# Two-block transformer step, first expert layer: results of 14 of its 16 experts placed by accumulating indirect DMA instead of by matrix products

## The chip, the cores and the metric

The kernel runs on one core of a Trainium2 chip; the other cores are idle. The metric is the device time of one execution in microseconds (us). Three executions of the kernel before took 3236.24, 3239.30 and 3238.56 us, median 3238.56. One more execution was profiled.

The core's engines work side by side: PE (matrix products, with its weight loads PEld), DVE (vector), ACT (scalar), POOL (GpSimd) and SP, which here only issues weight loads. Semaphores tie them together. All DMA queues of the core share 16 DMA engines.

## What is computed

The reference runs two layers of a hybrid attention block, then two layers of a second block. The change is in the expert stage of the second block's first layer (layer 0), where both the 512 latent tokens and the 256 context tokens go through 16 experts:

```python
def expert_choice_ffn(h, router_w, w_gate, w_up, w_down):
    B, n, D = h.shape                        # n = 512 (latent) or 256 (context), D = 1024
    cap = EC_CAPACITY * n // N_EXPERTS       # 64 or 32 tokens for each of 16 experts
    aff = jax.nn.softmax((h @ router_w).astype(F32), axis=-1)
    gate, idx = lax.top_k(jnp.swapaxes(aff, 1, 2), cap)
    xe = jax.vmap(lambda hb, ib: hb[ib])(h, idx)
    a = jnp.einsum('becd,edf->becf', xe, w_gate)
    u = jnp.einsum('becd,edf->becf', xe, w_up)
    ye = jnp.einsum('becf,efd->becd', jax.nn.silu(a) * u, w_down) * gate[..., None].astype(h.dtype)
    return jax.vmap(lambda ib, yb: jnp.zeros((n, D), h.dtype).at[ib.reshape(-1)].add(yb.reshape(-1, D)))(idx, ye)

lat = lat + mod_l[5] * expert_choice_ffn(h_l, ...)      # and the same for the context
```

Each expert picks its 64 best latent tokens; its 64 result rows are scaled by their gates and added into the rows of those tokens. A token can be picked by several experts, but only once by each. Everything is float32. The weights of one expert are three 1024 x 1024 matrices, 12 MB in all.

## The kernel before

The program is a row of phases. In each, every engine runs its own function, and semaphores (`S[...]`, `wait_ge`) order them; no scheduler moves anything. The residual stream lies turned in the memory of the core: `XT` holds it as 8 blocks of 128 channels by 512 tokens, `CT` the same for the context.

**Weights.** `Stream.load` (L275) on SP loads the weights in pieces of 1 MB, in the order in which PE uses them. In this layer a ring of 13 pieces is used, somewhat more than the 12 of one expert. A load waits until the piece that lay in its place is used (`w_used`). The ring's last two places hold the token rows before, so their first loads also wait until these are stored: `if OPENED[self.n] == FIRST_OPEN + 1: self.e.wait_ge(S["rows_kept"], 16 * 6)`.

**The gate phase.** `pool_first_gate` (L2467) stores the 768 token rows into the DRAM array `KEPT` (named token_rows in the trace), in six DMAs (L2477). `dve_top` and `dve_select` make selection matrices for four experts at a time.

**The expert loop on PE** (`pe_moe_both`, L2718). For an expert e: half of the context products (L2740), the latent products with gate and up weights (L2727), the other half of the context products; then `pe_turn` turns the hidden values (L2804), `pe_turn_ctx` the context's (L2797); then the down products, latent (L2770) and context (L2779). Between these stand small jobs, planned in `Moe.plan` (L1959) and issued by `pe_aux` (L2562) at two spots: (e, 0) lies between `pe_turn` and `pe_turn_ctx`, (e, 1) right before the down products. "first" and "last" lie before and behind the loop. The kinds of jobs:
- x, xc: the inputs of the next four experts, turned from rows that POOL gathered from `KEPT` (L2580); emptied by ACT.
- i: token numbers and gates of four experts as columns in PSUM (L2571, L2574); emptied by DVE (L2655 to L2662) into `SHARE` (gates), `PLACE` and `ROWS` (token numbers).
- y: the results of a pair of experts into all tokens, one job for each of the 8 blocks of channels. It is a product of the 128 result rows `YE` with a 128 x 512 matrix `G` that holds the gate where row and token belong together (L2601). DVE multiplies it by the modulation and adds it to `XT` (L2648).
- yc: the same for the context, four experts at a time (L2606, L2666).

The y jobs of a pair run during the two experts that come next, four in each, in experts 2 to 15; the eight of the last pair run in "last". The jobs at the inner spots take turns on three PSUM banks: `inner = (2, 3, 6) if s.ctx`. `pe_aux` waits until the job that last used the bank has been emptied.

**DVE** (`dve_moe_d`): `product` (L2868) multiplies the two halves of the hidden values, `copy` (L2863) and `product_ctx` (L2873) serve the context, `dve_aux` empties its jobs, `pair_map` (L2896) makes `G`. **ACT** (`act_moe_d`): the silu, the copy of the turned hidden values (L2829), and the copies of an expert's 64 result rows into `YE` (L2852), which end with `e_ready`. **POOL** (`pool_experts`): nine indirect gathers of 128 rows each (L2489), three for each of the groups 1 to 3 of four experts.

The second layer has a loop of its own, `pe_moe_d`, which keeps its y jobs.

## Time and profile before

| | |
|---|---|
| three executions, us | 3236.24, 3239.30, 3238.56 |
| the profiled execution, us | 3236.32 |
| its span from first to last instruction, us | 3234.5 |
| PE busy in the span | 3049.3 us, 94% |
| DVE, ACT, POOL busy | 47%, 22%, 10% |
| granted TensorE clock, mean | 0.981 of full speed |
| layer 0's expert loop, start of expert 0 to end of "last" | about 1801.8 to 2408.6 us |

The profile comes from one execution. Its span plus what lies around it is that execution's time, 3236.32 us, which is 2.24 us under the median of the three. Times in the rows are counted from the start of the span. A float32 product stands in the trace as two MATMUL instructions (a transposition as one), so the 128 y products of both layers are 256 instructions. An instruction's duration includes the time in which it overlaps its neighbours; the distance from start to start tells what it really costs.

### The profile page before, as it was taken

To read this page: it belongs to the slowest core of one execution; us is meant where nothing else is said; L and a number is where in the kernel's file an instruction comes from. 1 tells how busy PE (TensorE), PEld (TensorE's weight loads), DVE (VectorE), ACT (ScalarE), POOL (GpSimd) and SP (SyncE) were. 2 spreads that over 40 slices of the span, in tenths; PEclk is the share of its full clock that TensorE was granted. 3 is DMA by queue.
4 is the path that set the end of the run, shared out by engine and by line. 5 is a ranking of instruction groups with operands and counts; after the bars stand their busy time and mean duration, and the time that the engine had idled before them with its cause. 6 is when DMAs were issued, how large, how long until landed. Compare 5 with 4: busy or idle time off the path is not lost.

```text
span 3234.5 us, 36328 instructions
## 1 busy us (share of the span) xinstructions
PE 3049.3 (94%) x14559; PEld 1675.0 (52%) x14559; DVE 1526.7 (47%) x2852; ACT 726.6 (22%) x1521; POOL 330.1 (10%) x195
## 2 busy tenths in 40 slices
PE   8999899998989899999998999999999888899998
PEld 5888443787744344456755533333335544444443
DVE  5993942998482434765565222222243762111112
ACT  1211532121262211121124100000014652111111
POOL 4553000655200000000001000000000000000000
PEclk9999999999999899999999999999999999999999
DMA  5442003455201222010412798888841003999997
GB/s 221 169 183 96 10 1 125 158 192 225 79 1 39 106 81 107 33 52 30 161 65 93 331 376 338 351 343 331 348 176 52 27 3 138 379 421 421 421 421 294
DMA packets 87625, 598.23 MB, mean 185 GB/s; under 512 B 10456, under 2 KB 11259, under 8 KB 16932
## 3 DMA queue, kind: packets, MB, share of 16 engines
q1 hardware_dynamic: 79776, 575.70, 44.5%
q10 hardware_dynamic: 5524, 12.35, 1.1%
q0 software_dynamic: 2160, 7.87, 0.6%
q8 instruction: 117, 1.92, 0.2%
q14 instruction: 48, 0.39, 0.0%
HBM read 590.64 MB, written 5.24 MB: 184 GB/s over the span
## 4 chain that ended last, share of the span: by engine, by line
PE 63%; DVE 7%; ACT 2%; issue 1%; another core or an unknown queue 0%; DVEq 0%; ACTq 0%; PEldq 0%
PE ps L1358 8%; PE ps L2727 7%; PE ps L2689 7%; PE ps L2706 3%; PE ps L2770 3%; PE ps L2740 3%; PE ps L2601 3%; PE ps L1091 3%; PE ps L3013 2%; PE ps L2584 2%; PE ps L2779 2%; PE ps L2500 2%; PE ps L1456 2%; PE ps L1696 2%; PE ps L3174 1%; PE ps L1508 1%
## 5 line engine op out<-in xcount | busy, mean ns | idle before, releaser
L610 PE MATMUL ps<-mem 128*128 128x256 f32 x1792 | 393.3, 381 | 12.7 <-DVE mem L640 10.8
L610 PEld LDWEIGHTS ps<-mem 128*128 128x128 f32 x1792 | 340.2, 191 | 65.2 <-DVE mem L640 14.7
L555 POOL TENSOR_TENSOR mem<-mem 128x512 f32<-128x512 f32 (+1 forms) x160 | 302.0, 1887 | 544.4 <-DVE mem L851 284.8
L2868 DVE TENSOR_TENSOR mem<-ps,mem 128x512 f32<-128x512 f32 x32 | 22.1, 692 | 547.0 <-PE ps L2689 313.4
L753 DVE SCALAR_TENSOR_TENSOR mem<-mem 128x1024 f32<-128x1024 f32 x160 | 255.3, 1635 | 13.4 <-DMA mem<-in_ada_w 13.4
L1358 PE MATMUL ps<-mem 128*128 128x512 f32 (+1 forms) x768 | 253.5, 492 | 2.9 <-ACT mem L1199 2.9
L2727 PE MATMUL ps<-mem 128*64 128x512 f32 x1024 | 223.3, 594 | 0.0
L2689 PE MATMUL ps<-mem 128*64 128x512 f32 x1024 | 222.5, 592 | 0.7 <-ACT mem L2626 0.7
L1358 PEld LDWEIGHTS ps<-mem 128*128 128x128 f32 x768 | 147.1, 193 | 108.6 <-issue 97.2
L640 DVE TENSOR_TENSOR mem<-ps,mem 128x256 f32<-128x256 f32 x308 | 121.2, 418 | 111.8 <-PE ps L610 68.3
L1091 PE MATMUL ps<-mem 128*128 128x512 f32 x384 | 169.6, 597 | 1.8 <-DVEq L156 1.8
L2727 PEld LDWEIGHTS ps<-mem 128*64 128x64 f32 x1024 | 72.1, 137 | 150.5 <-issue 150.5
L2689 PEld LDWEIGHTS ps<-mem 128*64 128x64 f32 x1024 | 74.4, 137 | 145.6 <-issue 144.6
L608 PE MATMUL ps<-mem 128*128 128x256 f32 x672 | 146.3, 379 | 1.5 <-POOL mem L555 1.5
L608 PEld LDWEIGHTS ps<-mem 128*128 128x128 f32 x672 | 127.6, 190 | 19.2 <-issue 1.9
L2601 PE MATMUL ps<-mem 128*128 128x512 f32 x256 | 117.3, 596 | 1.7 <-ACT mem L2852 1.3
L1091 PEld LDWEIGHTS ps<-mem 128*128 128x128 f32 x384 | 71.5, 190 | 88.3 <-issue 85.6
L2740 PE MATMUL ps<-mem 128*32 128x512 f32 x1024 | 116.1, 594 | 0.0
L2706 PE MATMUL ps<-mem 128*64 128x512 f32 x512 | 113.4, 595 | 1.1 <-ACT mem L2829 1.1
L2770 PE MATMUL ps<-mem 128*64 128x512 f32 x512 | 113.4, 595 | 0.0
L2648 DVE SCALAR_TENSOR_TENSOR mem<-ps,mem 128x512 f32<-128x512 f32 x128 | 96.0, 750 | 33.2 <-PE ps L2601 22.2
L2852 ACT ACTIVATE mem<-ps 64x512 f32<-64x512 f32 x64 | 37.9, 592 | 294.2 <-PE ps L2770 153.9
(412 smaller groups left out, 4071.5 us busy)
## 6 DMA issues: line engine op xcount, KB each, us to landing
mem<-in_moe_w SPq DMA_DIRECT2D x384, 1024.0 KB, 14.0
mem<-in_w_in SPq DMA_DIRECT2D x48, 1024.0 KB, 8.3
mem<-in_ada_w SPq DMA_DIRECT2D x48, 1024.0 KB, 4.9
mem<-in_hy_w_in SPq DMA_DIRECT2D x24, 1024.0 KB, 7.0
mem<-in_w_out SPq DMA_DIRECT2D x12, 1024.0 KB, 6.9
mem<-in_k_win_l SPq DMA_DIRECT2D x8, 1024.0 KB, 6.9
mem<-in_hy_w_out SPq DMA_DIRECT2D x8, 1024.0 KB, 4.9
mem<-in_sw_w_in SPq DMA_DIRECT2D x6, 1024.0 KB, 7.2
```

Source lines behind the costliest of these rows:

```text
L555: gp(out, x, y, op).then_inc(A.mark(sem), 1)
L608: m = mm(seven(l, unit), y[:, k, u * P:(u + 1) * P], x[:, k, :], start=(k == 0), stop=(k == 3))
L610: m = mm(seven(l, unit), x[:, k, :], y[:, k, :], start=(k == 0), stop=(k == 3))
L753: stt(PRODUCT if again else w, w, 1.0, C_ROWS[:, z, :], ALU.mult, ALU.mult, accum_out=mod(layer, b // KD, b % KD, z))\
L1091: m = mm(ps[:, b, :], Wr[slot[n]][:, k, b * P:(b + 1) * P], GT[:, 4 * c + k, :], start=(n == 0 and k == 0), stop=(n == 2 and k == 3))
L1358: m = mm(ps[:, j % 4, 0:L], Wc[s][:, k, (j % 4) * P:(j % 4 + 1) * P], H[:, k, :], start=(k == 0), stop=(k == KD - 1))
L2601: m = mm(ps[:, bank, :], m_.YE[i % len(m_.YE)][:, j * P:(j + 1) * P], m_.G, start=True, stop=True)
L2689: m = mm(ps[64 * x:64 * x + 64, part, :], lat(k), w[x][:, k % 4, :], start=(k == 0), stop=(k == KD - 1))
L2706: m = mm(ps[64 * x:64 * x + 64, 7, :], m_.AT[:, k, :], w[x][:, k % 4, :], start=(k == 0), stop=(k == KD - 1))
L2727: m = mm(ps[64 * x:64 * x + 64, part, :], m_.XS[e // GROUP % 2][:, k, e % GROUP, 0:CAP_L], w[x][:, k % 4, :], start=(k == 0), stop=(k == K ...
L2740: m = mm(ps[32 * i:32 * i + CAP_C, 4, :], m_.XS[e // GROUP % 2][:, k, e % GROUP, CAP_L:], w[i][:, k % 4, :], start=(k == 0), stop=(k == KD ...
L2770: m = mm(ps[64 * x:64 * x + 64, 7, :], m_.AT[:, k, :], w[k // 4 * 2 + x][:, k % 4, :], start=(k == 0), stop=(k == KD - 1))
```

## The change

1. In layer 0 the y jobs of pairs 0 to 6 (experts 0 to 13) are gone: 56 jobs. The eight of pair 7 stay in "last".
2. POOL, after the six stores of token rows, sets a tile to zero and stores it four times into a new DRAM array `ADDED` (512 x 1024). SP's wait on `rows_kept` and POOL's now include these four stores.
3. For each of experts 0 to 13, `add_rows` issues one indirect DMA on POOL: the 64 rows of `YE` are added to 64 rows of `ADDED`, whose numbers stand in the new `TARGET`. It waits for the expert's `e_ready` and for the add before it. The gathers of groups 2 and 3 stand in POOL's order before the adds of experts 3 and 7.
4. After the last add POOL loads `ADDED` into four tiles `BACK`. Eight new "back" jobs in expert 15 (two at (15, 0), six at (15, 1)) turn them, four transpositions each, and DVE adds each to `XT` by the instruction that empties a y job.
5. In layer 0 `product` multiplies by the gate, which now has a row for each slot in the new `GATE`; it was `tensor_tensor` and is `scalar_tensor_tensor`, with a wait on DVE's own last instruction. `G` holds ones in place of gates. Emptying an i job takes 19 tiny instructions in place of 11, and the i job of experts 0 to 3 moves from (0, 1) to "first".
6. ACT writes experts 0 to 13 alternately into two `YE` tiles, always in partitions 0 to 63, and waits from expert 2 to 14 for the add of the expert two before.

PE, one expert of the layer's loop in the middle (expert 4). Before:

```order
L2740 MATMUL ps<-mem 32x512 x16
L2804 MATMUL ps<-mem 128x128 x4
L2580 MATMUL ps<-mem 128x128 x4
L2797 MATMUL ps<-mem 128x128 x4
L2601 MATMUL ps<-mem 128x512 x4
L2606 MATMUL ps<-mem 128x256 x2
L2770 MATMUL ps<-mem 64x512 x16
```

The same place in the changed kernel, whose lines are numbered anew (L2840 is `pe_turn`, L2609 the x job, L2833 `pe_turn_ctx`, L2639 yc, L2806 the down products):

```order
L2776 MATMUL ps<-mem 32x512 x16
L2840 MATMUL ps<-mem 128x128 x4
L2609 MATMUL ps<-mem 128x128 x4
L2833 MATMUL ps<-mem 128x128 x4
L2639 MATMUL ps<-mem 128x256 x2
L2806 MATMUL ps<-mem 64x512 x16
```

The four y products have gone and nothing has taken their place.

PE at the end of the layer, from the last hidden products of expert 15. Before:

```order
L2740 MATMUL ps<-mem 32x512 x16
L2804 MATMUL ps<-mem 128x128 x4
L2601 MATMUL ps<-mem 128x512 x2
L2797 MATMUL ps<-mem 128x128 x4
L2601 MATMUL ps<-mem 128x512 x2
L2606 MATMUL ps<-mem 128x256 x2
L2770 MATMUL ps<-mem 64x512 x16
L2779 MATMUL ps<-mem 32x512 x16
L2601 MATMUL ps<-mem 128x512 x8
L2606 MATMUL ps<-mem 128x256 x8
```

The same place in the changed kernel (L2634 are the "back" transpositions, L2630 the y products that stay):

```order
L2776 MATMUL ps<-mem 32x512 x16
L2840 MATMUL ps<-mem 128x128 x4
L2634 MATMUL ps<-mem 128x128 x8
L2833 MATMUL ps<-mem 128x128 x4
L2634 MATMUL ps<-mem 128x128 x24
L2639 MATMUL ps<-mem 128x256 x2
L2806 MATMUL ps<-mem 64x512 x16
L2815 MATMUL ps<-mem 32x512 x16
L2630 MATMUL ps<-mem 128x512 x8
L2639 MATMUL ps<-mem 128x256 x8
```

Four products make way for 32 transpositions; "last" is as it was.

POOL, from the stores of token rows to the end of the layer in the changed kernel (before, only the rows of token_rows stood here, the nine gathers one behind another):

```order
L2483 DMA token_rows<-mem 128x1024 x6
L2485 MEMSET mem 128x1024
L2488 DMA added_rows<-mem 128x1024 x4
L2518 DMA mem<-token_rows,mem 128x1024 x3
L2496 DMA added_rows<-mem 512x1024 x3
L2518 DMA mem<-token_rows,mem 128x1024 x3
L2496 DMA added_rows<-mem 512x1024 x4
L2518 DMA mem<-token_rows,mem 128x1024 x3
L2496 DMA added_rows<-mem 512x1024 x7
L2508 DMA mem<-added_rows 128x1024 x4
```

The gathers (L2518) of groups 2 and 3 now stand behind three and seven adds (L2496). The diff, cut to its core:

```diff
 S["stored"] = ctx.enter_context(nc.semaphore("stored"))
-for n in ("rows_kept", "rows_in0", "rows_in1", "rows_in2"):
+for n in ("rows_kept", "rows_in0", "rows_in1", "rows_in2", "rows_added"):
     S[n] = ctx.enter_context(nc.semaphore(n))
 KEPT = nc.dram_tensor("token_rows", (T + TC, D), F32, kind="Internal").ap()
+ADDED = nc.dram_tensor("added_rows", (T, D), F32, kind="Internal").ap()
 for turn, sems in zip("ab", S.sets):
...
 if OPENED[self.n] == FIRST_OPEN + 1:
-    self.e.wait_ge(S["rows_kept"], 16 * 6)
+    self.e.wait_ge(S["rows_kept"], 16 * 10)
 self.e.dma_start(v(SLOT_AT[s], WCH), src).then_inc(S[f"w_in{s}"], 16)
...
 TOK_, IDF_, IDU_, GA_ = (LS_ + 12 * i for i in range(4))
-assert DEPTH * N_LV >= 48
+GE_, IDE_ = LS_ + 48, LS_ + 64
+assert DEPTH * N_LV >= 80
 one = Map(AR_)
...
 GROUP = 4
-AUX_ENGINE = {"x": "act", "xc": "act", "g": "act", "i": "dve", "y": "dve", "yc": "dve"}
+AUX_ENGINE = {"x": "act", "xc": "act", "g": "act", "i": "dve", "y": "dve", "yc": "dve", "back": "dve"}
 OUTER_BANKS = (3, 0, 1, 2)
...
 s.ROWS = M[:, IDU_:IDU_ + 12].bitcast(U32)
+s.GATE = v(GE_, N_EXP)
+s.TARGET = M[0:64, IDE_:IDE_ + N_EXP].bitcast(U32)
+s.BACK = [v(at, 1024) for at in (HNC_, HNC_ + 1024, KEPT_, SEL_)]
 s.KEPT = [v(at, 1024) for at in (HNC_, HNC_ + 1024, KEPT_)]
...
     s.put("first", OUTER_BANKS, "i", 1)
+    s.put("first", (2,), "i", 0)
 for e in range(N_EXP):
...
         more = group + 1 < s.groups
-        ys = [("y", pair - 1, 4 * (e % 2) + k) for k in range(4)] if pair else []
-        ahead = [("x", group + 1, i)] if more else ys[:2]
-        after = ys if more else ys[2:]
+        back = [("back", 0, k) for k in range(KD)] if e == N_EXP - 1 else []
+        ahead = [("x", group + 1, i)] if more else back[:2]
+        after = back[2:]
         if more and i % 2:
...
             after.append(("yc", group - 1, i))
-        if e in (0, 2, 6):
-            after.append(("i", {0: 0, 2: 2, 6: 3}[e], 0))
+        if e in (2, 6):
+            after.append(("i", {2: 2, 6: 3}[e], 0))
     else:
...
         A.e.dma_start(KEPT[t * P:(t + 1) * P, :], rows).then_inc(S["rows_kept"], 16)
+    zeros = MOES[0].KEPT[2]
+    nc.gpsimd.memset(zeros, 0.0).then_inc(A.mark(), 1)
+    A.e.wait_ge(*A.last)
+    for t in range(4):
+        A.e.dma_start(ADDED[t * P:(t + 1) * P, :], zeros).then_inc(S["rows_kept"], 16)
 
 def pool_experts(A, m_):
 
-    A.e.wait_ge(S["rows_kept"], 16 * 6)
-    for group in range(1, m_.groups):
-        A.e.wait_ge(*m_.evacuated(m_.jobs.index(("i", group, 0))))
-        for which in range(3):
-            if group > 1:
-                last = ("xc", group - 1, 1) if which == 2 else ("x", group - 1, 2 * which + 1)
-                A.e.wait_ge(S["aux_full"], m_.jobs.index(last) + 1)
-            at = 3 * group + which
-            nc.gpsimd.indirect_dma_start(m_.KEPT[which], None, KEPT, bass.IndirectOffsetOnAxis(m_.ROWS[:, at:at + 1], 0))\
-                .then_inc(S[f"rows_in{which}"], 16)
+    def add_rows(e):
+        A.e.wait_ge(S["e_ready"], e + 1)
+        if e:
+            A.e.wait_ge(S["rows_added"], 16 * e)
+        nc.gpsimd.indirect_dma_start(ADDED, bass.IndirectOffsetOnAxis(m_.TARGET[:, e:e + 1], 0), m_.YE[e % 2][0:64, :], None,
+                                     compute_op=ALU.add).then_inc(S["rows_added"], 16)
+
+    A.e.wait_ge(S["rows_kept"], 16 * 10)
+    gather_group(A, m_, 1)
+    for e in range(N_EXP - 2):
+        if e in (3, 7):
+            gather_group(A, m_, (e + 1) // 4 + 1)
+        add_rows(e)
+    A.e.wait_ge(S["rows_added"], 16 * (N_EXP - 2))
+    A.e.wait_ge(S["aux_full"], m_.jobs.index(("xc", 3, 1)) + 1)
+    for t in range(4):
+        A.e.dma_start(m_.BACK[t], ADDED[t * P:(t + 1) * P, :]).then_inc(S["rows_kept"], 16)
+
+def gather_group(A, m_, group):
+
+    A.e.wait_ge(*m_.evacuated(m_.jobs.index(("i", group, 0))))
+    for which in range(3):
+        if group > 1:
+            last = ("xc", group - 1, 1) if which == 2 else ("x", group - 1, 2 * which + 1)
+            A.e.wait_ge(S["aux_full"], m_.jobs.index(last) + 1)
+        at = 3 * group + which
+        nc.gpsimd.indirect_dma_start(m_.KEPT[which], None, KEPT, bass.IndirectOffsetOnAxis(m_.ROWS[:, at:at + 1], 0))\
+            .then_inc(S[f"rows_in{which}"], 16)
 
...
     if m_.ctx:
-        A.e.wait_ge(S["pair_map"], i + 1)
+        A.e.wait_ge(S["pair_map"], 1)
     else:
         A.e.wait_ge(*m_.evacuated(m_.jobs.index(("g", i, 0))))
-    m = mm(ps[:, bank, :], m_.YE[i % len(m_.YE)][:, j * P:(j + 1) * P], m_.G, start=True, stop=True)
+    m = mm(ps[:, bank, :], m_.YE[0][:, j * P:(j + 1) * P], m_.G, start=True, stop=True)
+elif kind == "back":
+    A.e.wait_ge(S["rows_kept"], 16 * 14)
+    for t in range(4):
+        m = tr(ps[:, bank, t * P:(t + 1) * P], m_.BACK[t][:, j * P:(j + 1) * P], IDENT)
 else:
...
 A.e.wait_ge(*A.last)
-if kind == "y":
+if kind in ("y", "back"):
     stt(XT[:, j, :], ps[:, bank, :], mod(m_.layer, 5, j, 0), XT[:, j, :], ALU.mult, ALU.add)\
...
         for r in range(2):
-            at = 18 * u + 2 + 4 * i + 2 * u + r
-            copy(m_.SHARE[64 * r:64 * r + 64, i, u:u + 1], ps[64 * r:64 * r + 64, bank, at:at + 1]).then_inc(A.mark(), 1)
+            e, at = 4 * i + 2 * u + r, 18 * u
+            rows = ps[64 * r:64 * r + 64, bank, :]
+            for half in range(2):
+                copy(m_.GATE[64 * half:64 * half + 64, e:e + 1], rows[:, at + 2 + e:at + 3 + e]).then_inc(A.mark(), 1)
+            copy(m_.TARGET[:, e:e + 1], rows[:, at:at + 1]).then_inc(A.mark(), 1)
     for r in range(4):
...
 r = 64 * (e % 2)
+YE = m_.YE[e // 2 % len(m_.YE)]
+if m_.ctx and e < N_EXP - 2:
+    r, YE = 0, m_.YE[e % 2]
+elif m_.ctx:
+    YE = m_.YE[0]
+if m_.ctx and 2 <= e < N_EXP - 1:
+    A.e.wait_ge(S["rows_added"], 16 * (e - 1))
 for dh in range(2):
-    act(m_.YE[e // 2 % len(m_.YE)][r:r + 64, dh * 512:(dh + 1) * 512], ps[64 * dh:64 * dh + 64, 7, :], ACT.Copy)\
+    act(YE[r:r + 64, dh * 512:(dh + 1) * 512], ps[64 * dh:64 * dh + 64, 7, :], ACT.Copy)\
         .then_inc(A.mark("e_ready" if dh else None), 1)
...
 A.e.wait_ge(S["psum_full"], 2 * e + 2)
-tt(m_.HID, ps[:, 1, :], m_.HID, ALU.mult).then_inc(A.mark("c_ready"), 1)
+if m_.ctx:
+    A.e.wait_ge(*A.last)
+    stt(m_.HID, ps[:, 1, :], m_.GATE[:, e:e + 1], m_.HID, ALU.mult, ALU.mult).then_inc(A.mark("c_ready"), 1)
+else:
+    tt(m_.HID, ps[:, 1, :], m_.HID, ALU.mult).then_inc(A.mark("c_ready"), 1)
 
...
 def pair_map(pair):
-    if pair:
-        A.e.wait_ge(S["aux_full"], m_.jobs.index(("y", pair - 1, KD - 1)) + 1)
     g, u = pair // 2, pair % 2
-    ts(m_.G, m_.IO, m_.PLACE[:, g, u:u + 1], m_.SHARE[:, g, u:u + 1], ALU.is_equal, ALU.mult)\
-        .then_inc(A.mark("pair_map"), 1)
+    ts(m_.G, m_.IO, m_.PLACE[:, g, u:u + 1], None, ALU.is_equal).then_inc(A.mark("pair_map"), 1)
 
...
     select({1: 2, 4: 3}[e])
-if e % 2:
-    A.e.wait_ge(*A.last)
+if e == N_EXP - 1:
     pair_map(e // 2)
```

## Rows read from the trace of the kernel before

**Rows 1.** The page: busy time by engine, and one of its costliest groups.

```profile
PE 3049.3 (94%) x14559; PEld 1675.0 (52%) x14559; DVE 1526.7 (47%) x2852; ACT 726.6 (22%) x1521; POOL 330.1 (10%) x195
...
L555 POOL TENSOR_TENSOR mem<-mem 128x512 f32<-128x512 f32 (+1 forms) x160 | 302.0, 1887 | 544.4 <-DVE mem L851 284.8
```

**Rows 2.** Windows from expert to expert (0, 1, 3, 4, 13, 14, 15), then "last".

```profile
core 0: us, PE busy (x) PEld busy (x) DVE busy (x) ACT busy (x) POOL busy (x), PEclk, DMA share, GB/s
1801.75:1836.86 35.11, 35.11 (x226) 13.21 (x229) 4.88 (x25) 3.15 (x6) 2.92 (x3) 1.00 1.01 421
1836.86:1870.24 33.38, 33.38 (x213) 11.34 (x208) 6.83 (x14) 3.70 (x7) 0.00 (x0) 1.00 1.01 421
...
1908.76:1945.59 36.83, 36.83 (x221) 12.64 (x217) 8.42 (x13) 3.74 (x7) 1.87 (x2) 1.00 0.93 370
1945.59:1982.83 37.24, 37.24 (x220) 13.07 (x216) 10.17 (x19) 3.15 (x6) 0.00 (x0) 1.00 0.85 341
...
2284.25:2321.05 36.80, 36.80 (x217) 12.61 (x212) 8.97 (x14) 2.76 (x5) 0.00 (x0) 1.00 0.85 343
2321.05:2357.85 36.80, 36.80 (x216) 12.61 (x212) 8.42 (x13) 2.77 (x5) 0.00 (x0) 1.00 0.85 343
2357.85:2394.90 37.05, 36.99 (x216) 12.48 (x208) 9.30 (x15) 2.76 (x5) 0.00 (x0) 1.00 0.66 256
2394.90:2409.40 14.50, 10.65 (x32) 5.51 (x33) 12.97 (x22) 0.77 (x2) 0.00 (x0) 1.00 0.00 0
```

**Rows 3.** The chain of waits in 1790 to 2420: start, us, what.

```profile
1854.36 3.57 PE ps L2740 x32
1859.83 7.02 PE ps L2770 x32
```

**Rows 4.** Timeline, end of expert 15: start, us, engine, instructions, idle before.

```profile
2378.85 0.66 PE L2804 MATMUL ps<-mem 128*128 128x128 f32 x4
2378.99 0.69 DVE L2863 COPY mem<-ps 128x512 f32<-128x512 f32 x1 [2.83 <-PE ps L2740]
...
2379.35 1.88 PE L2601 MATMUL ps<-mem 128*128 128x512 f32 x4
2379.55 0.60 ACT L2829 ACTIVATE mem<-ps 128x512 f32<-128x512 f32 x1 [6.99 <-PE ps L2804]
2380.41 1.61 DVE L2648 SCALAR_TENSOR_TENSOR mem<-ps,mem 128x512 f32<-128x512 f32 x2 [0.73 <-PE ps L2601]
2381.07 0.60 PE L2797 MATMUL ps<-mem 128*128 128x128 f32 x4
2381.50 1.88 PE L2601 MATMUL ps<-mem 128*128 128x512 f32 x4
...
2382.12 0.42 DVE L2873 TENSOR_TENSOR mem<-mem,ps 128x256 f32<-128x256 f32 x1
...
2383.22 1.03 PE L2606 MATMUL ps<-mem 128*128 128x256 f32 x4
2384.18 7.09 PE L2770 MATMUL ps<-mem 128*64 128x512 f32 x32
```

**Rows 5.** Waits in 1880 to 2450: engine, line, waited for: us, times, longest.

```profile
DVE mem L2868 <- PE ps L2727: 203.3, 14, 14.5
ACT mem L2852 <- PE ps L2770: 138.8, 14, 13.0
```

**Rows 6.** DMA queues in expert 1 (1836.86 to 1870.24): packets, MB, share.

```profile
q1 hardware_dynamic: 1926, 14.03, 101.0%
```

**Rows 7.** DMA queues in expert 0 (1801.75 to 1836.86), q0 the three gathers.

```profile
q1 hardware_dynamic: 1811, 13.17, 89.9%
q0 software_dynamic: 432, 1.57, 11.2%
```

**Rows 8.** DMA queues in expert 14 (2321.05 to 2357.85).

```profile
q1 hardware_dynamic: 1728, 12.58, 85.3%
```

**Rows 9.** Line L2489, the gathers on POOL (128 rows each).

```profile
L2489 POOL DMA_INDIRECT mem<-token_rows,mem x9: 936/937/995, 1804.5 to 2084.9; - x9
...
DMA to landing us min/median/max: 5.7/9.9/13.9
```

**Rows 10.** Line L2477, the stores of token rows, the same columns.

```profile
L2477 POOL DMA_DIRECT2D token_rows<-mem x6: 531/536/725, 1759.0 to 1777.1; - x6
...
DMA to landing us min/median/max: 2.9/3.0/3.9
```

**Rows 11.** Timeline of SP around the start of the layer.

```profile
1795.14 4.69 SPq L289 DMA_DIRECT2D mem<-in_moe_w  x9
```

**Rows 12.** Timeline of DVE, PE and POOL in expert 0.

```profile
1801.85 0.72 DVE L2655 COPY mem<-ps 64x1 f32<-64x1 f32 x4 [4.21 <-PE ps L2574]
...
1804.48 0.99 POOL L2489 DMA_INDIRECT mem<-token_rows,mem  x1 [26.80 <-DVE mem L2662]
...
1819.39 0.69 DVE L2868 TENSOR_TENSOR mem<-ps,mem 128x512 f32<-128x512 f32 x1 [15.75 <-PE ps L2727]
...
1822.77 0.65 PE L2804 MATMUL ps<-mem 128*128 128x128 f32 x4
1823.26 0.60 PE L2580 MATMUL ps<-mem 128*128 128x128 f32 x4
```

## The prediction

> **What bounds the kernel now.** I read the page's busy times first, then one window for each expert of layer 0, the chain of waits in that stage, its waits by engine, the DMA queues, and last the timeline where the change works. PE is busy 94% of the span, the next engine 47% [rows 1]. Inside the expert loop PE is busy for the whole of every window, 35.11 of 35.11 us and so on, at full clock [rows 2], and the chain runs from one PE group to the next [rows 3]. DVE and ACT wait for PE there, not PE for them [rows 5]. The DMA engines are the only other thing near a limit: a share of 1.01 and 421 GB/s in experts 0 and 1, but 0.85 and about 341 GB/s from expert 4 on [rows 2]. So in this stage a PE product that leaves is worth its full distance from start to start, until DMA becomes the limit. The later phases depend on this one only through when it ends, so what is won here should reach the end.
>
> **Removed: 56 y products.** Experts 1 and 3 have the same jobs but for four y jobs in expert 3. Their windows are 33.38 and 36.83 us [rows 2], so four y jobs cost 3.45 us, 0.86 us each. The changed kernel lacks them in 14 experts: 14 x 3.45 = 48.3 us. PE is never idle there, so all of it is on the path. The DVE additions that go with them (1.61 us for two [rows 4]) are off the path and count for nothing.
>
> **Added: eight "back" jobs in expert 15.** Four groups of four transpositions (the two turns, x, xc) lie between the end of the hidden products, 1854.36 + 3.57 = 1857.93, and the down products at 1859.83 [rows 3]: 0.48 us a group. On PE alone eight back jobs cost 3.8 us. But DVE needs 0.80 us for each (1.61 for two [rows 4]), and only three banks take turns. With T as the start of the turn, 2378.85 before: DVE's context copy ends at T + 0.83; back 0 and 1 run on DVE to about T + 2.7; the context product takes 0.42, to T + 3.1; back 2 to 5 end at T + 6.3. The context job yc uses the bank of back 5, so PE starts it there, and it takes 0.96 us (2383.22 to 2384.18): the down products start at T + 7.3. Before they started at T + 5.33 [rows 4], of which the y jobs were 3.45. The back jobs therefore add 7.3 - 1.9 = 5.4 us. Ends: 3.8 us (PE alone), and 8 x 0.80 = 6.4 with nothing overlapped. I take 5.4.
>
> **A cover that goes.** In experts 12 to 14 the two y jobs at (e, 0) have no successor there, so `pe_turn_ctx` stands right behind `pe_turn`. It needs DVE's context copy, which ends 2379.68 - 2378.85 = 0.83 us after the turn starts, while the turn takes 0.50 [rows 4]. With a semaphore's delay that is about 0.4 us of new idle time, three times: 1.2 us (0 to 2). In the other experts an x job stands between. Expert 1 has run without y jobs already, and its 1.90 us for four groups show no wait [rows 3]; so the turned hidden values' way over ACT, 0.60 us [rows 4], is hidden too.
>
> **Edits that I cost at nothing.** The gated `product`: L2868 lasts 0.69 us, and the new form is that of L2648, 0.80; it starts at 1819.39 and the turn that needs it stands at 1822.77 [rows 12], behind the second half of the context products, which cover it, and the wait on DVE's own last instruction is for something long done. The i jobs' eight extra copies take 8 x 0.18 = 1.5 us (0.72 for four [rows 12]). In "first" both i jobs are emptied before expert 0's product, 1801.85 + 2 x 3.3 = 1808.5 against 1819.39; the first gather goes out 1.5 us late, 1806 in place of 1804.48, lands 5.7 to 13.9 us later [rows 9] and is wanted at 1823.26. The moved i job itself takes as long on PE before expert 0 as it took inside it. POOL's zeros: the last token row store goes out at 1777.1 [rows 10]. The memset isn't in the trace; between 0 and 4 us, nearest a POOL instruction on 512 columns at 1.89 [rows 1], doubled. Four issues of 0.54 us each, landing in 3.0 to 3.9 [rows 10], end near 1789, and SP issues its nine weight loads at 1795.14 [rows 11], when the DMA queues stood idle. If that margin were used up, only the last two of the nine would wait. Gathers of groups 2 and 3 now stand behind adds 2 and 6, which are issued when their expert ends; the rows are wanted a whole expert, 33 us, later. ACT's new wait is for an add issued a whole expert earlier; behind it on ACT stand `e_ready` and PE's next down products. `BACK`: add 13 can start at the end of expert 13, the transpositions come after expert 14 and the hidden part of 15, about 33 + 21 us later, for one add and four loads.
>
> **DMA load of the adds.** The nearest row: three gathers, 384 rows of 4 KB, take 11.2% of 35.11 us on all engines, 1.31 us each [rows 7]. An add of 64 rows at that price is 0.66 us; if it reads its destination and costs three passes, 2.0 us. Spare: twelve pieces, 12.58 MB [rows 8], need 29.9 us at the rate of expert 1, 14.03 MB in 33.38 us [rows 6], the nine gathers (11.8 us over experts 0 to 11) about 1.0 an expert, and PE will need 33.4 or more. 33.4 - 29.9 - 1.0 = 2.5 us. Both ends fit, the upper by 0.5 us. I take 1.3 us an add, and no wait.
>
> **Sum.** -48.3 + 5.4 + 1.2 = -41.7 us. From the profiled execution: 3236.3 - 41.7 = 3194.6 us. That execution was 2.2 us below the median of the runs; between the two, I say 3196. Its own range, from the ends of the terms and the 3 us by which runs differ: 3191 to 3200.
>
> **Rivals.**
> A. DMA becomes the limit because accumulating rows is dear. For it: 1.01 of share with 421 GB/s shows a hard ceiling, and only 2.5 us are spare; nothing in the trace has ever accumulated. Against: 64 rows are few. At 5 us an add: 12 experts x (5 - 2.5) = 30 us given back, 3225; at 3.5 us, 12 back, 3207. I take 3212. Chance 12%.
> B. Slower: the chain of adds. Each waits for the one before, and ACT may not overwrite `YE` until the add of two experts before has landed. Once an add takes longer from issue to landing than an expert on PE, the experts run at its pace; from 36.9 us on, more than is won. At 45 us: 14 x (45 - 36.9) - 7 or so = +107, 3340; at 40 us 3275. The same place turns against the change if DMA time per add passes 2.5 + 3.45 = 6 us. Against: a gather of twice the bytes lands in 5.7 to 13.9 us beside full weight traffic [rows 9]. Chance 4%.
> C. The loads are hidden but a smaller loss appears: PE waits for `BACK` in expert 15, or the first weights wait for the zeros. 10 us lost at one place, 3206. Against: margins of some 40 and 5 us above. Chance 6%.
> D. The weights stream more slowly than I count. 12.58 MB at a lower rate would need 35.1 us, with gathers and adds about 37: no gain but in experts 12 to 14, some 5 us, 3231. Both windows at 421 GB/s speak against it [rows 2], and 1%. The Trainium skill's page "DMA: Bandwidth & Descriptors", section "Bandwidth" (Where 436 GB/s comes from), says that loads from HBM are bound by about 358 GB/s for a core; the 35.1 us are 12.58 MB at that figure. By that rule this rival would hold; the trace disagrees, with 421 GB/s read for a whole expert.
> E. The change doesn't do what it says: y products that stay on PE. The order of instructions rules it out; under 1%.
>
> **Chances.** Forecast 77%; A 12, C 6, B 4, D and E 1. The range reaches from 3189 into A: 3189 to 3209, which leaves about 7% above from A, 4 from B, 1 from D and some 5 for surprises at either side. What a measurement of this kernel can tell from no change is about 0.2%, 6.5 us. Faster by more: the forecast, C, most of A and 0.5 of D, 93%. Within: 3%. Slower: 4%.
>
> **What would show it.** Windows of 33.4 us for expert 3, 33.8 for 4 and 13, 35.1 for 2; PE still busy all through; a DMA share of 0.93 to 0.97. In expert 15 the down products 7.3 us behind the turn, with PE waiting for DVE at L2634. About 0.4 us of idle time at `pe_turn_ctx` in experts 12 to 14. Landing of an add under 14 us. If A holds, PE waits for DMA on `in_moe_w` in the hidden products and share stays at 1.01; if B holds, ACT waits for a DMA at the `YE` copies. The prediction is wrong if expert windows stay above 35 us.

## The result

| | before | changed |
|---|---|---|
| median of four executions, us | 3238.93 (3236.24 to 3241.47) | 3200.12 (3197.49 to 3201.88) |
| the profiled execution, us | 3236.32 | 3201.88 |
| PE busy, us | 3049.3 | 3013.6 |
| gate phase's first products to the first product behind layer 0 (the stage), us | 687.38 | 649.62 |

The changed kernel takes 0.988 of the time of before, 95% interval 0.9863 to 0.9897: 38.8 us less. Forecast were 3196 us and a range of 3189 to 3209.

The last row is a measure that I use for all kernels below, under the name stage, since it lies around the change and nothing else: from the first group of 16 products of the gate phase on PE (3.72 us long; at 1722.03 before, 1725.18 in the changed kernel) to the first product of the phase behind layer 0 (2409.41 and 2374.80). It is 37.76 us shorter. The profiled execution of the changed kernel reached the gate phase 3.15 us later than that of before, in code that the change doesn't touch; over the thirteen profiled executions below that time lies between 1721.2 and 1727.4 us, whatever the kernel, and such differences blur medians by 2 to 3 us. Behind the stage the two executions take the same: 825.11 us before, 825.09 in the changed kernel. So what the change wins in the stage reaches the end.

### The profile page after: what moved, and what is told of

It reads as the page before. It is cut to its first block, busy times and chain, and to the rows that moved or that the text cites. A ratio compares the mean times of both kernels' runs of the same rounds, so it can differ in the third digit from the quotient of the medians.

```text
span 3199.9 us, 36092 instructions
## 1 busy us (share of the span) xinstructions
PE 3013.6 (94%) x14479; PEld 1659.9 (52%) x14479; DVE 1491.0 (47%) x2829; ACT 726.0 (23%) x1521; POOL 355.5 (11%) x218
## 4 chain that ended last, share of the span: by engine, by line
PE 62%; DVE 7%; ACT 2%; issue 1%; DMA 0%; another core or an unknown queue 0%; DVEq 0%; SPq 0%; ACTq 0%; PEldq 0%
PE ps L1359 8%; PE ps L2763 7%; PE ps L2725 7%; PE ps L2776 4%; PE ps L2742 4%; PE ps L2806 4%; PE ps L1092 3%; PE ps L3056 2%; PE ps L2613 2%; PE ps L2815 2%; PE ps L2529 2%; PE ps L1457 2%; PE ps L2630 2%; PE ps L1697 2%; PE ps L3217 1%; PE ps L1509 1%
## 5 line engine op out<-in xcount | busy, mean ns | idle before, releaser
L1092 PE MATMUL ps<-mem 128*128 128x512 f32 x384 | 169.6, 597 | 1.8 <-DVEq L156 1.8
L2915 DVE TENSOR_TENSOR mem<-ps,mem 128x512 f32<-128x512 f32 x16 | 11.1, 692 | 314.1 <-PE ps L2725 314.1
L2913 DVE SCALAR_TENSOR_TENSOR mem<-ps,mem 128x512 f32<-128x512 f32 x16 | 12.0, 751 | 232.4 <-PE ps L2763 232.4
L2806 PE MATMUL ps<-mem 128*64 128x512 f32 x512 | 113.4, 595 | 0.0
L1873 POOL TENSOR_TENSOR mem<-mem 128x512 f32<-128x512 f32 x8 | 10.1, 1266 | 860.1 <-ACT mem L1746 860.1
L2859 ACT ACTIVATE mem<-ps 128x512 f32<-128x512 f32 x32 | 19.1, 597 | 352.8 <-PE ps L2763 262.0
```

Of the source, the lines that this page charges most:

```text
L1092: m = mm(ps[:, b, :], Wr[slot[n]][:, k, b * P:(b + 1) * P], GT[:, 4 * c + k, :], start=(n == 0 and k == 0), stop=(n == 2 and k == 3))
L2806: m = mm(ps[64 * x:64 * x + 64, 7, :], m_.AT[:, k, :], w[k // 4 * 2 + x][:, k % 4, :], start=(k == 0), stop=(k == KD - 1))
```

## The profile after

The page of the changed kernel, the line that answers to [rows 1].

```profile
PE 3013.6 (94%) x14479; PEld 1659.9 (52%) x14479; DVE 1491.0 (47%) x2829; ACT 726.0 (23%) x1521; POOL 355.5 (11%) x218
```

Windows of the changed kernel, with the columns of [rows 2]: the end of the gate phase with "first", then experts 0 to 4, 13, 14, 15 and "last".

```profile
1784.00:1808.67 24.67, 23.85 (x136) 20.95 (x134) 10.93 (x40) 5.70 (x17) 1.59 (x3) 0.92 0.49 194
1808.67:1843.29 34.62, 34.62 (x205) 11.15 (x208) 5.65 (x30) 3.14 (x6) 4.42 (x4) 0.95 1.02 422
1843.29:1876.68 33.39, 33.39 (x213) 11.35 (x209) 6.35 (x13) 3.70 (x7) 1.46 (x1) 1.00 1.02 414
1876.68:1911.76 35.08, 35.08 (x228) 13.19 (x224) 7.39 (x26) 3.14 (x6) 1.55 (x2) 1.00 0.99 391
1911.76:1945.15 33.39, 33.39 (x213) 11.34 (x209) 4.93 (x8) 3.70 (x7) 4.22 (x4) 1.00 0.99 384
1945.15:1978.96 33.81, 33.81 (x213) 11.56 (x208) 7.23 (x15) 3.14 (x6) 1.43 (x1) 1.00 1.02 414
...
2253.35:2287.16 33.81, 33.58 (x208) 11.12 (x204) 5.48 (x9) 2.76 (x5) 1.41 (x1) 1.00 0.98 381
2287.16:2320.97 33.81, 33.58 (x208) 11.12 (x204) 5.48 (x9) 2.76 (x5) 2.29 (x4) 1.00 1.00 399
2320.97:2360.28 39.31, 38.14 (x240) 14.45 (x232) 12.12 (x19) 2.76 (x5) 0.00 (x0) 1.00 0.71 286
2360.28:2375.00 14.72, 10.85 (x40) 5.71 (x44) 13.18 (x22) 0.97 (x2) 0.00 (x0) 1.00 0.00 0
```

Expert 3 fell from 36.83 to 33.39 us, expert 4 from 37.24 to 33.81, experts 13 and 14 from 36.80 to 33.81. PE is still busy in all of them, but for 0.23 us each in experts 13 and 14; DMA share rose from 0.93 in expert 3 and 0.85 in the others to between 0.98 and 1.02. Two windows carry a clock below 1.00, "first" and expert 0, where before stood 1.00 for expert 0. So the whole way from before to after can be added up by windows: "gate to expert 0" +3.77 us (of which the moved i job 2.2), expert 0 -0.49, expert 1 +0.01, experts 2 to 14 together from 487.61 (1870.24 to 2357.85) to 444.29 us, -43.32, expert 15 up to its down products +2.27; behind these 0.00 (25.23 us from the down products to the end of the stage in both); sum -37.76.

The timeline of the end of expert 15 answers to [rows 4]: start, us, engine, instructions, idle time before.

```profile
2341.98 0.66 PE L2840 MATMUL ps<-mem 128*128 128x128 f32 x4
2342.11 0.69 DVE L2906 COPY mem<-ps 128x512 f32<-128x512 f32 x1 [2.78 <-PE ps L2776]
...
2343.11 1.61 DVE L2681 SCALAR_TENSOR_TENSOR mem<-ps,mem 128x512 f32<-128x512 f32 x2 [0.30 <-PE ps L2634]
...
2345.14 5.02 DVE L2681 SCALAR_TENSOR_TENSOR mem<-ps,mem 128x512 f32<-128x512 f32 x6
2345.95 0.66 PE L2634 MATMUL ps<-mem 128*128 128x128 f32 x4 [0.52 <-DVE mem L2681]
2346.80 0.66 PE L2634 MATMUL ps<-mem 128*128 128x128 f32 x4 [0.20 <-DVE mem L2681]
...
2349.57 7.09 PE L2806 MATMUL ps<-mem 128*64 128x512 f32 x32
```

The down products start 7.59 us behind the turn (5.33 before). The transpositions come 0.85 us apart, each behind a wait for DVE's addition to `XT`: DVE's pace, through the three banks. And in expert 14, the context turn:

```profile
2308.16 0.66 PE L2840 MATMUL ps<-mem 128*128 128x128 f32 x4
2308.30 0.69 DVE L2906 COPY mem<-ps 128x512 f32<-128x512 f32 x1 [2.78 <-PE ps L2776]
...
2309.05 0.66 PE L2833 MATMUL ps<-mem 128*128 128x128 f32 x4 [0.23 <-DVE mem L2906]
```

It starts 0.89 us behind the turn, not 0.49: the 0.4 us that lost their cover, 0.23 of them idle time. Line L2496, the adds, and the software queue in expert 1 (one add):

```profile
L2496 POOL DMA_INDIRECT added_rows<-mem x14: 1408/1427/1482, 1841.4 to 2285.5; - x14
...
DMA to landing us min/median/max: 6.2/8.2/8.8
```

```profile
q0 software_dynamic: 80, 0.26, 3.9%
```

An add lands within 8.8 us, far from the 33 us of an expert, and takes the DMA engines 3.9% of 33.39 = 1.30 us, where 64 gathered rows took 0.66, half of what 128 took [rows 7]. The one thing in this profile that no step of the forecast had is the clock. PE at the start of the layer in the changed kernel, then the same place before:

```profile
1782.54 13.30 PE L2305 MATMUL ps<-mem 128*128 128x256 f32 x48
...
1804.20 1.86 PE L2600 MATMUL ps<-mem 128*128 128x18 f32 x16
1805.91 0.60 PE L2603 MATMUL ps<-mem 128*128 128x18 f32 x4
1806.36 1.94 PE L2600 MATMUL ps<-mem 128*128 128x18 f32 x16
1808.14 0.60 PE L2603 MATMUL ps<-mem 128*128 128x18 f32 x4
1808.67 5.29 PE L2776 MATMUL ps<-mem 128*32 128x512 f32 x32
```

```profile
1779.40 11.75 PE L2299 MATMUL ps<-mem 128*128 128x256 f32 x48
...
1799.51 1.86 PE L2571 MATMUL ps<-mem 128*128 128x18 f32 x16
1801.22 0.60 PE L2574 MATMUL ps<-mem 128*128 128x18 f32 x4
1801.75 3.64 PE L2740 MATMUL ps<-mem 128*32 128x512 f32 x32
```

Expert 0's first context products take 5.29 in place of 3.64 us, and the gate's 48 products 13.30 in place of 11.75. Windows cut to just these stretches give the granted clock, 0.68 and 0.79 in the changed kernel, 1.00 and 0.89 before:

```profile
1808.67:1813.96 5.29, 5.29 (x35) 1.23 (x36) 3.78 (x27) 0.00 (x0) 2.68 (x3) 0.68 1.02 431
...
1782.54:1795.84 13.30, 13.30 (x50) 10.95 (x50) 7.38 (x21) 1.69 (x5) 1.66 (x4) 0.79 0.42 165
```

```profile
1801.75:1805.39 3.64, 3.64 (x35) 1.01 (x36) 1.54 (x11) 0.00 (x0) 0.91 (x1) 1.00 1.02 423
...
1779.40:1791.15 11.75, 11.75 (x50) 9.88 (x50) 7.38 (x21) 1.69 (x5) 0.00 (x0) 0.89 0.02 9
```

A mean below 1.00 means that part of the stretch ran at the lower of TensorE's two levels, 1.2 in place of 2.4 GHz. Together the two stretches cost 3.2 us. Whether the change causes them, one profile can't say.

## The experiments

Theories at the start. Bound: PE bounds the loop, y jobs are worth 0.86 us each and nothing takes their place until DMA demand exceeds PE's. Rival: DMA already limits the changed kernel, as its share of 1 suggests. Clock: the two i jobs in a row, now both in "first", bring a spell at 1.2 GHz; rival: the spells come by chance. Banks: the 7.6 us of expert 15 are a matter of PSUM banks.

| kernel | median, us | kernel before beside it | stage, us | behind it, us | expert 0's first products | gate's 48 products |
|---|---|---|---|---|---|---|
| before | | | 687.38 | 825.1 | 3.64 | 11.75 |
| changed | 3200.12 | 3238.93 | 649.62 | 825.1 | 5.29 | 13.30 |
| no y jobs | 3194.00 | 3239.43 | 642.65 | 825.4 | 3.64 | 13.30 |
| i job moved, alone | 3240.27 | 3239.43 | 690.75 | 825.1 | 5.46 | 11.7 |
| i job in mid-expert | 3200.59 | 3239.43 | 648.20 | 826.4 | 3.64 | 13.28 |
| five banks | 3202.09 | 3239.43 | 647.98 | 827.0 | 5.45 | 11.71 |
| no adds | 3202.17 | 3239.02 | 649.61 | 825.3 | 5.41 | 11.67 |
| five adds an expert | 3238.27 | 3239.02 | 688.01 | 824.3 | 5.29 | 13.31 |
| no back jobs | 3197.52 | 3239.02 | 644.46 | 827.1 | 5.50 | 11.77 |
| mid-expert and five banks | 3197.96 | 3239.02 | 644.91 | 826.5 | 3.64 | 11.70 |
| i jobs apart | 3199.82 | 3239.60 | 646.51 | 825.1 | 3.64 | 11.79 |
| changed, again | 3200.65 | 3239.60 | 649.60 | 825.1 | 5.39 | 11.65 |
| mid-expert and five banks, again | 3197.57 | 3239.60 | 645.06 | 826.5 | 3.64 | 11.80 |

All columns from "stage" on come from one profiled execution of each kernel, in us; "behind it" is the time from the end of the stage to the end of the span.

**The y jobs alone.** The kernel before with

```diff
-ys = [("y", pair - 1, 4 * (e % 2) + k) for k in range(4)] if pair else []
+ys = []
...
-if pair:
-    A.e.wait_ge(S["aux_full"], m_.jobs.index(("y", pair - 1, KD - 1)) + 1)
```

> The kernel before without the y jobs of pairs 0 to 6 (the results of experts 0 to 13 are left out of the sum), nothing else changed. Term of the prediction: 56 jobs x 0.86 us = 48.3 us less, and 0.4 us of new idle time in each of experts 12 to 14, also 0.4 in expert 15: 46 to 48 us below the kernel before. Expert windows as in the changed kernel: 33.39, 33.8, 34.25 us. Rival (the y jobs hid waits for weights or for DVE in every expert): less than 40 us, with windows longer than the changed kernel's. The first products of expert 0 stay at full clock, since the i job of experts 0 to 3 has not moved.

Measured: 45.4 us less, ratio 0.9852 (0.9837 to 0.9867); stage 44.73 us shorter, though this execution had the longer gate products (+1.55), so 46.3 without that. The forecast was 46 to 48: the stage without the slower gate products lies inside, the median 0.6 us short of it. The distances between experts are those of the changed kernel (33.39, 33.81, 34.25 us), and expert 0's first products ran at full clock. The term for the removed work stands.

**The adds.** The changed kernel without its 14 accumulating DMAs and the waits on `rows_added`:

```diff
-nc.gpsimd.indirect_dma_start(ADDED, bass.IndirectOffsetOnAxis(m_.TARGET[:, e:e + 1], 0), m_.YE[e % 2][0:64, :], None,
-                             compute_op=ALU.add).then_inc(S["rows_added"], 16)
```

> The changed kernel without the 14 accumulating DMAs (and without the waits for them), so that zeros are read back: the results of experts 0 to 13 are left out of the sum. Theory PE bound: the adds cost nothing, expert windows stay 33.39, 33.81 and 34.25 us, time within 2 us of the changed kernel (3200); only the DMA share falls, from 1.02 to about 0.98 in expert 4. Rival A of the prediction (DMA already is the limit in part): windows shorter than these, 5 us or more gained.

Stage 649.61 against 649.62 us in the changed kernel and 649.60 in its repeat, whose clock ran most like this one's (5.39 and 11.65 us in the last two columns); 3202.17 us in all. Expert 4:

```profile
1947.13:1980.94 33.81, 33.81 (x212) 11.57 (x208) 7.23 (x15) 3.14 (x6) 0.00 (x0) 1.00 1.00 402
```

The window is 33.81 us as with adds; the share fell only from 1.02 to 1.00. So the adds cost nothing, and the rival falls. A DMA share of 1 with PE busy all through is not a limit reached here. The program issues each load as early as its place comes free, and PE waits for none; that waiting in the queues is what fills the share is my reading of it, not shown.

**Where DMA does become the limit.** Five adds an expert, to five arrays (the waits on `rows_added` count all five):

```diff
-nc.gpsimd.indirect_dma_start(ADDED, bass.IndirectOffsetOnAxis(m_.TARGET[:, e:e + 1], 0), m_.YE[e % 2][0:64, :], None,
-                             compute_op=ALU.add).then_inc(S["rows_added"], 16)
+for dst in [ADDED] + MORE:
+    nc.gpsimd.indirect_dma_start(dst, bass.IndirectOffsetOnAxis(m_.TARGET[:, e:e + 1], 0), m_.YE[e % 2][0:64, :], None,
+                                 compute_op=ALU.add).then_inc(S["rows_added"], 16)
```

> The changed kernel with five adds for each expert in place of one, to five different DRAM arrays, so that DMA gets 4 x 1.30 = 5.2 us more work in each of 14 experts; ACT and POOL wait for all five of an expert. Theory: an add costs the DMA engines 1.30 us (queue share 3.9% of 33.39 us), twice a plain transfer; demand per expert 29.9 + 6.5, and 1.0 for gathers, is 36.4 to 37.4 us, above PE's 33.8. DMA becomes the limit: windows of 36 to 37.5 us, PE waits for in_moe_w, 25 to 40 us slower than the changed kernel, 3225 to 3240. If an add's true DMA cost is lower (the share counts waiting), windows stay below 35 and the loss below 15 us. If the adds' latency sets the pace, ACT waits for the adds before L2895's copies instead.

3238.27 us, ratio to before 0.9998 (0.9988 to 1.0007): 38 us back, the whole gain. Experts 4 and 5, and what PE waits for (from the list of waits: us in total, times, longest):

```profile
1945.05:1983.62 38.57, 36.16 (x208) 12.34 (x209) 5.95 (x14) 3.15 (x6) 5.90 (x5) 0.96 1.02 386
1983.62:2019.68 36.06, 34.46 (x212) 12.09 (x213) 5.78 (x11) 3.70 (x7) 7.10 (x6) 1.00 1.03 387
```

```profile
PE ps L2778 <- DMA mem<-in_moe_w: 20.2, 9, 4.0
PE ps L2765 <- DMA mem<-in_moe_w: 6.1, 8, 1.2
```

Experts 3 to 14 take (2354.72 - 1908.87) / 12 = 37.15 us each, 3.05 more than in the changed kernel (34.10), 36.6 us in all. PE's waits for `in_moe_w` make 26.3 us of that. The clock reads 0.96 in the first window and 0.98 over experts 6 to 14, where the changed kernel has 1.00: spells at 1.2 GHz came too. Whether they added to the loss or stood in place of waits for weights isn't shown. The demand forecast from 1.30 us an add was 36.4 to 37.4. An add landed in 7.6 to 14.5 us, so it isn't the chain of adds that sets the pace; no wait of ACT for a DMA stands in the list. The share reads 1.02 and 1.03, the changed kernel's 1.02: share alone hardly tells the two apart, PE's waits for `in_moe_w` do.

**The back jobs.** The changed kernel with `back = []` and without the four loads of `BACK`.

> The changed kernel without the four loads of the added rows and without the eight back jobs: the results of experts 0 to 13 are left out of the sum. Prediction's term: back jobs cost 5.4 us (5.7 by the profile of the changed kernel, 7.6 - 1.9); without them turn to down products in expert 15 takes 2.3 us (0.4 of it the wait for DVE's context copy), 5.3 us less. Whole kernel 5 us below the changed one, 3195.

Stage 644.46, 5.16 us less than the changed kernel; turn to down products 2340.41 - 2338.07 = 2.34 us, from 7.59: 5.25. Against the repeat of the changed kernel, whose gate products and spell were like those here, the stage is 5.14 us shorter. The median is 2.6 us under the changed kernel's, where 5 were forecast. Executions of one kernel differ by 4 us and more, so the median can't tell 2.6 from 5. But the profiled execution also took 827.1 us behind the stage in place of 825.1: 2 of the 5 us didn't reach the end there (see under banks).

**Banks.** The changed kernel with

```diff
+turn = [2, 3, 6, 1, 5, 2, 3, 6, 1]
 for job in ahead:
-    s.put((e, 0), inner, *job)
+    s.put((e, 0), (turn.pop(0),) if s.ctx and e == N_EXP - 1 else inner, *job)
...
+if e == N_EXP - 1:
+    A.e.wait_ge(*m_.evacuated(m_.jobs.index(("back", 0, KD - 1))))
```

> The changed kernel with five PSUM banks (2, 3, 6, 1, 5) for the nine jobs of expert 15 instead of three. Theory banks: PE waits in expert 15 only because a bank is handed back at DVE's pace of 0.84 us a job; with five banks the down products start about 5.8 us behind the turn, not 7.6, and the kernel is 1.8 us faster than the changed one. Rival: DVE's work shifts behind and something else waits for it (the context down products need bank 5 empty, the last jobs need DVE), so that the 1.8 us come back as a wait before L2815 or in the last jobs.

```profile
2341.53 0.66 PE L2845 MATMUL ps<-mem 128*128 128x128 f32 x4
...
2343.33 2.83 PE L2637 MATMUL ps<-mem 128*128 128x128 f32 x24
2346.36 1.13 PE L2642 MATMUL ps<-mem 128*128 128x256 f32 x4 [0.20 <-DVE mem L2684]
2347.42 7.09 PE L2809 MATMUL ps<-mem 128*64 128x512 f32 x32
```

5.89 us in place of 7.59, and six jobs run without a wait; "last" is unchanged. The stage is 1.64 us shorter. But the median, 3202.09, isn't lower. Four executions can't settle 1.8 us, but the profile shows where the gain went in this execution. PE right behind the stage, in the changed kernel and then here:

```profile
2374.80 3.28 PE L418 MATMUL ps<-mem 128*32 128x128 f32 x64 [3.58 <-ACT mem L401]
...
2397.35 1.97 PE L418 MATMUL ps<-mem 128*64 128x128 f32 x32
```

```profile
2372.65 3.64 PE L418 MATMUL ps<-mem 128*32 128x128 f32 x64 [3.58 <-ACT mem L401]
...
2396.62 1.97 PE L418 MATMUL ps<-mem 128*64 128x128 f32 x32
```

From the first of these groups to the second it is 22.55 us there and 23.97 here, and the granted clock over the first 15 us is 0.77 there and 0.58 here. So 1.42 of the 1.64 us were given back within 25 us of the stage's end, where the clock was lower. The column "behind it" shows a like loss for mid-expert, for no back jobs and for mid-expert with five banks (twice): 1.3 to 2.0 us longer than in the changed kernel. It isn't there for i jobs apart, nor for the change itself (825.11 and 825.09). What decides it isn't shown.

**The clock: the i job alone.** The kernel before with the i job moved as the change moves it:

```diff
     s.put("first", OUTER_BANKS, "i", 1)
+    s.put("first", (2,), "i", 0)
...
-if e in (0, 2, 6):
+if e in (2, 6):
```

> The kernel before with only the i job of experts 0 to 3 moved ahead of expert 0, behind the other i job. Theory clock: the two i jobs in a row, 40 products of 18 columns in 4.5 us, are followed by a spell of half clock in expert 0's first context products, which then take 5.3 in place of 3.6 us; whole kernel 1.6 us slower than before. Rival chance: the spell in the changed kernel's profile belongs to that execution or to how far its phases have shifted; no spell there, no difference. A window of row times tells; the difference of medians is at the limit of what 5 rounds can tell.

```profile
1800.89 1.86 PE L2572 MATMUL ps<-mem 128*128 128x18 f32 x16
1802.60 0.60 PE L2575 MATMUL ps<-mem 128*128 128x18 f32 x4
1803.05 2.99 PE L2572 MATMUL ps<-mem 128*128 128x18 f32 x16
1805.87 1.02 PE L2575 MATMUL ps<-mem 128*128 128x18 f32 x4
1806.82 5.46 PE L2741 MATMUL ps<-mem 128*32 128x512 f32 x32
```

The spell is there, and here began already inside the second i job (2.99 for 1.86 us). The stage took 3.37 us more. The medians, 3240.27 of 11 and 3239.43, differ by less than they can tell (ratio 1.0002, 0.9993 to 1.0011).

**Mid-expert.** The changed kernel with the i job of experts 0 to 3 between the two halves of expert 0's hidden products:

```diff
-s.put("first", (2,), "i", 0)
+s.put("mid", (2,), "i", 0)
...
 lat(e, 0)
 st.next(4)
+if e == 0:
+    pe_aux(A, m_, "mid")
...
 dve_aux(A, m_, "first")
+dve_aux(A, m_, "mid")
```

> The changed kernel with the i job of experts 0 to 3 issued in the middle of expert 0's hidden products, behind the first halves, instead of right behind the other i job. Theory clock: no half clock spell at expert 0's first context products (3.6 us for L2776's first group of 32, not 5.3), 1.6 us less than the changed kernel, 3198 to 3199 if that one is at 3200. Rival chance: the spell appears or not whatever the order; no difference.

No spell; stage 648.20, 1.42 us shorter, and 1.35 us more behind it; the medians (3200.59 against 3200.12) show nothing.

**Apart.** The same products ahead of expert 0, in the order xc, xc, i, xc, xc, i:

```diff
 for i in range(4):
-    s.put("first", OUTER_BANKS, "xc" if s.ctx else "x", 0, i)
+    s.put("first", ((3, 0, 2, 1)[i],) if s.ctx else OUTER_BANKS, "xc" if s.ctx else "x", 0, i)
+    if s.ctx and i == 1:
+        s.put("first", (3,), "i", 0)
 if s.ctx:
-    s.put("first", OUTER_BANKS, "i", 1)
-    s.put("first", (2,), "i", 0)
+    s.put("first", (2,), "i", 1)
```

> The changed kernel with the two i jobs of 'first' apart: two xc jobs, the i job of experts 0 to 3, the two other xc jobs, then the i job of experts 4 to 7. The same products before expert 0 in another order. Theory: the half clock spell ahead of and in expert 0's first context products needs the two i jobs in a row (4.5 us of products with 18 columns); apart, no spell there, stage from the gate's start to the next phase 1.4 to 1.6 us shorter than in the changed kernel (649.6 us), 648.1. Rival: it is the amount of narrow products before expert 0 that counts, in whatever order; then a spell of 3.4 or 6.8 us starts within 5 us of expert 0's first product here too.

```profile
1802.32 1.86 PE L2601 MATMUL ps<-mem 128*128 128x18 f32 x16
...
1806.34 1.86 PE L2601 MATMUL ps<-mem 128*128 128x18 f32 x16
1808.04 0.60 PE L2604 MATMUL ps<-mem 128*128 128x18 f32 x4
1808.57 3.64 PE L2777 MATMUL ps<-mem 128*32 128x512 f32 x32
```

No spell, and a stage of 646.51 us, 3.1 less than the changed kernel, of which the gate's products were faster by 1.5 in this profile against the first one of the changed kernel. Against the repeat of the changed kernel, which had them fast as well (649.60), all 3.1 us are the spell: it also lay on the second i job there. The expectation had only 1.4 to 1.6 us, taken from the shorter spell of the first profile.

**The clock, taken together.** Seven profiles are of kernels with both i jobs in a row: in all seven expert 0's first products are slowed, to 5.29 to 5.50 us. Six are of kernels without: in all six they take 3.64. The spell belongs to the change. The slower gate products (13.3 us in four profiles, 11.7 to 11.8 in nine) come with and without it, in the kernel without y jobs, which has none of the new code, as well; nothing in these thirteen profiles ties that part to the change, and I call it chance.

**Both edits, beside the changed kernel.** The mid-expert place and the five banks together, twice; the second time in one series with the changed kernel.

> The changed kernel with both of the edits tried before: the i job of experts 0 to 3 in the middle of expert 0's hidden products, and five banks for the nine jobs of expert 15. In the stage itself 1.4 + 1.7 = 3.1 us less than the changed kernel from the gate's start to the first products of the next phase; 3197 if it all reaches the end. Rival: the clock gives half of it back, since the spells of half clock at the phase borders lengthen or shorten by 3.4 us with where the border falls; then no difference in the medians that 5 rounds can tell.

> The changed kernel itself once more, to compare with the next kernel on the same chip: 3200, expert windows 33.39 and 33.81 us, a half clock spell of 3.4 or 6.8 us at expert 0's first context products.

> The kernel with both edits once more, beside the changed kernel: no half clock spell at expert 0, turn to down products of expert 15 in 5.9 us instead of 7.6; 3 us less in the stage, and medians 2 to 4 us apart, 3197 against 3200. Rival: borders of later phases give it back, medians within 1 us.

Stage 644.91 and 645.06 us against 649.60; medians 3197.96 and 3197.57 against 3200.65. The forecast for the medians was 2 to 4 us; 3.1 came. In the stage 3 were forecast and 4.5 to 4.7 came, since the spell that goes cost 3.1 us in the changed kernel beside it, not 1.4; behind the stage 1.4 us were given back. Executions scatter by 3 to 7 us, so the medians alone would be weak, but the stage with what lies behind it says the same: 3.3 and 3.1 us less. In this best version the whole change is worth 41 to 42 us.

## Why the prediction was right

By its own steps:
- Removed products: -48.3 forecast. With experts 2 to 14 the window sum fell by 43.32, where 13 x 3.45 less 1.2 for the lost cover gives 43.65. Right, and shown by the kernel without y jobs.
- Lost cover: 0.40 us seen where 0.4 were forecast, in experts 12 to 14 and only there.
- Back jobs: 5.4 us forecast, 5.7 by the profile (7.59 - 1.88), 5.2 to 5.3 when taken away, since without them a context copy shows. DVE's pace came out at 0.85 us a job, not 0.80; right mechanism, 0.3 us short.
- Adds: 1.3 us of DMA time each and no wait: both measured so (1.30 us, and 0.01 us of difference without them). The 1.3 was a choice between 0.66 and 2.0 us with no row behind it; that it came out to the digit is luck, and by the spare time measured anything between the ends would have given the same time. The spare time was somewhat too small: 5.2 us more DMA work made an expert 3.05 us longer, so together with the 1.3 about 3.45 us fit into 34.1. The forecast had 2.5 us for an expert of 33.4, which makes 3.2 for 34.1.
- Zeros: the memset took 0.97 us, bounded at 0 to 4; nothing waited for the stores.
- The moved i job was costed at nothing ("takes as long on PE before expert 0 as it took inside it"). This is the step that failed: its products took as long, but two such jobs in a row were followed by a spell at 1.2 GHz, 1.65 us in the profiled execution and up to 3.4 in others. The sum had no term for the clock at all.

The stage came out at -37.76 where -41.7 were forecast: 1.65 for that spell, 1.55 for the slower gate products, which are chance, 0.3 for DVE's pace, 0.3 in the y jobs' windows and 0.1 of rounding. The main cause was right and is shown; rivals A and B didn't come, and the five-fold adds show that A's mechanism is real, from about 3.45 us of adds an expert on.

The median, 3200.12 us, lies 4 us above the 3196 and just outside 3191 to 3200, the range that the forecast's own terms gave. It is well inside the stated range only because that reached up to 3209 for rival A, which didn't come; that much is luck. Rival B's 3340 should read about 3345 by its own terms (14 x (45 - 36.9) - 7 = 106 us); nothing else hangs on it.

Of the signs, the windows came as said (33.39, 33.81 and, for expert 2, 35.08 us), as did PE's waits for DVE at L2634, the 0.4 us, and the landings. The DMA share did not: 0.93 to 0.97 were forecast, 0.98 to 1.02 came. The prediction had named a share that stays at 1.01 as one of A's two signs; only the other, PE waiting for `in_moe_w`, told the two apart.

Of the clock the Trainium skill's page "TensorE: Matmul & The Clock Gate", section "Part 1: The HAM clock gate", says that it follows how busy PE has been recently. By the profile PE was busy without a gap through both i jobs (1804.20 to 1808.67), and 23.85 of the 24.67 us up to expert 0; with xc jobs of 128 columns between the i jobs the clock didn't fall. If busy means the profile's busy time, by that rule the changed kernel would have kept 2.4 GHz and the stage would have come out 1.65 us shorter; in that reading the trace doesn't agree with it. Why the clock falls there stays open.

## What to carry to other kernels

Where PE is busy without a gap, as it was here, products that leave are worth their start-to-start distance, and two neighbouring windows that differ only in them give that number before anything is changed. Moving a scatter-add from matrix products to accumulating DMA paid here as long as weights plus adds stayed under PE's time, and an add took the DMA engines twice the time of a gather of as many rows; look at PE's waits for weights, not at the DMA share, to know which side of that you are on. A gain in one phase can be partly given back by the clock at the start of the next, so read also what lies behind the stage. When small narrow products are moved together, look at the granted clock behind them, and spread them.

## What the runs showed of the hardware

- An accumulating indirect DMA of 64 rows of 4 KB into DRAM takes 1.30 us of all 16 DMA engines beside weight traffic, against 0.66 for 64 gathered rows (half of what 128 took), lands in 6.2 to 8.8 us, and occupies POOL for 1.41 to 1.48 us at issue, against 0.94 to 1.02 for a gather of 128 rows (changed kernel).
- DMA share reads 0.98 to 1.02 where PE waits for no weights (changed kernel) and 1.02 to 1.03 where 37 us are lost (five adds).
- Forty products of 18 columns in 4.5 us, PE busy throughout, were followed by a spell at 1.2 GHz in seven profiles of seven; with 2 us of products of 128 columns between them, in none of one, and with one i job alone in none of five.
- Over the 15 us behind the stage the granted clock read 0.77 before and in the changed kernel and 0.58 with five banks, whose next 25 us took 1.42 us longer for the same products.
